# The order of six class bodies behind an expert loop, on one core

## What is computed

```python
logits = (xf @ w_router + b_router)
top_val, top_idx = lax.top_k(logits, 4)          # 4 of 32 experts for each token
top_w = jax.nn.softmax(top_val, axis=-1)
# for each expert e, on the tokens that chose it:
hu = x[toks] @ w_up[e] + b_up[e]                 # 1024 -> 2048
ys = clamped_swiglu(hu) @ w_down[e] + b_down[e]  # 1024 -> 1024
out[tok] += gate * ys
```

## Time and profile before

| | |
|---|---|
| median of 3 runs | 1301.96 us (1298.96 to 1302.73) |
| profiled execution | 1302.53 us, span 1300.2 us |
| TensorE busy (MATMUL) | 1126.4 us, 87% |
| TensorE weight load | 572.4 us, 44% |
| VectorE, ScalarE | 316.0 and 314.6 us, 24% each |
| DMA | 464.88 MB, mean 358 GB/s |
| instruction queues | q8: 30 packets, 0.49 MB; q14: 9 packets, 0.07 MB |

### The profile page before, as it was taken

How to read it: one execution, slowest core, us unless ns; L and a number is a source line. 1 busy time by engine, 2 the same in 40 slices (tenths; PEclk the granted TensorE clock), 3 DMA queues, 4 the chain that set the end, 5 groups by cost and what they waited for, 6 DMA issues and landing times.

```text
span 1300.2 us, 20883 instructions
## 1 busy us (share of the span) xinstructions
PE 1126.4 (87%) x7942; PEld 572.4 (44%) x7943; DVE 316.0 (24%) x802; ACT 314.6 (24%) x589; POOL 0.2 (0%) x4
## 2 busy tenths in 40 slices
PE   6999899997999669988998989989978678687785
PEld 4745688844344334434343333443433333333332
DVE  3045444463112110311211211222111112111112
ACT  2145422132122221112222122231222112221213
POOL 0000000000000000000000000000000000000000
PEclk9999999997999899989999999999999999899898
DMA  9932754453899999559999999999999999999996
GB/s 379 427 125 97 287 230 172 196 217 129 306 390 428 429 427 409 194 193 429 426 428 429 428 428 428 428 428 428 428 429 429 427 430 427 428 428 428 429 429 269
DMA packets 33739, 464.88 MB, mean 358 GB/s; under 512 B 4002, under 2 KB 4130, under 8 KB 5540
## 3 DMA queue, kind: packets, MB, share of 16 engines
q1 hardware_dynamic: 32688, 460.98, 84.7%
q10 hardware_dynamic: 1012, 3.34, 0.6%
HBM read 463.25 MB, written 1.05 MB: 357 GB/s over the span
## 4 chain that ended last, share of the span: by engine, by line
PE 58%; DMA 37%; DVE 2%; issue 2%; ACT 0%; SPq 0%; DVEq 0%; ACTq 0%
DMA ring<-in_w_up 32%; PE psum L973 19%; PE psum L596 17%; PE psum L1050 8%; PE psum L901 4%; DMA ring<-in_w_down 4%; PE psum L965 2%; PE psum L1068 2%; DMA ring<-in_ada_quarters 1%; PE psum L662 1%; DVE area L1756 1%; PE psum L602 1%; PE psum L948 1%; PE psum L1010 0%; PE psum L799 0%
## 5 line engine op out<-in xcount | busy, mean ns | idle before, releaser
L973 PE MATMUL psum<-ring,area 128*32 128x512 f32 (+2 forms) x2432 | 389.0, 628 | 75.7 <-DMA ring<-in_w_up 75.6
L973 PEld LDWEIGHTS psum<-ring,area 128*32 128x32 f32 (+2 forms) x2432 | 107.1, 122 | 347.5 <-issue 226.9
L1050 PE MATMUL psum<-ring,area 128*32 128x256 f32 (+2 forms) x2080 | 191.4, 419 | 24.8 <-DVE area L1741 14.8
L901 PEld LDWEIGHTS psum<-area,x_res 128*128 128x128 f32 x1056 | 125.6, 198 | 34.5 <-issue 34.5
L901 PE MATMUL psum<-area,x_res 128*128 128x128 f32 x1056 | 132.6, 285 | 2.5 <-DVE area L1637 1.7
L1050 PEld LDWEIGHTS psum<-ring,area 128*32 128x32 f32 (+2 forms) x2080 | 75.9, 115 | 129.7 <-issue 66.3
L1263 ACT ACTIVATE area<-area 128x256 f32<-128x256 f32 x51 | 21.3, 417 | 415.4 <-DVE area L1716 415.4
L1716 DVE TENSOR_SCALAR area<-psum 128x256 f32<-128x256 f32 x51 | 21.6, 424 | 400.6 <-PE psum L973 400.6
L1222 ACT ACTIVATE area<-psum,mod,small 128x128 f32<-128x128 f32 (+1 forms) x272 | 101.5, 454 | 60.0 <-PE psum L901 58.6
L1251 ACT ACT_TABLE_LOAD x32 | 41.1, 1283 | 290.2 <-PE psum L948 290.2
L596 PE MATMUL psum<-ring,hT 128*128 128x512 f32 (+1 forms) x192 | 77.5, 559 | 0.0
(11 more groups left out here) (201 smaller groups left out, 655.7 us busy)
## 6 DMA issues: line engine op xcount, KB each, us to landing
ring<-in_w_up SPq DMA_DIRECT2D x128, 2048.0 KB, 22.2
ring<-in_w_down SPq DMA_DIRECT2D x64, 2048.0 KB, 22.5
ring<-in_w_in SPq DMA_DIRECT2D x10, 2048.0 KB, 16.0
ring<-in_ada_w SPq DMA_DIRECT2D x8, 2048.0 KB, 13.7
ring<-in_ada_quarters SPq DMA_DIRECT2D x4, 2048.0 KB, 18.3
ring<-in_w_out SPq DMA_DIRECT2D x2, 2048.0 KB, 9.8
ring<-in_w_in SPq DMA_DIRECT2D x4, 512.0 KB, 19.1
ring<-in_w_branch_b SPq DMA_DIRECT2D x1, 2048.0 KB, 9.3
```

Of the source, the lines that this page charges most:

```text
L901: ins = pe.matmul(ps[banks[i]][:, kk % 4 * P:(kk % 4 + 1) * P], x3[:, tt, kk * P:(kk + 1) * P], S[:, tt, 0:P], start=(tt == 0 and kk % 4 = ...
L973: ins = pe.matmul(ps[b][g * P // G:(g + 1) * P // G, 0:w], XT[:, kk, t0:t0 + P // G], wt[:, c0:c0 + w], start=False, stop=kk == KT - 1, sk ...
L1050: ins = pe.matmul(ps[b][g * M:(g + 1) * M, 0:w], hidT[:, p, q * P + of * M:q * P + (of + 1) * M], down_weights(kk)[:, g * W + d * CW:g * W ...
```

## The change

One tuple gets another order. All bodies, their instructions and the order of the turns stay as they are; only the places of the class bodies in the programs of TensorE, ScalarE and VectorE move. Class 2 (96 tokens) now follows the loop, then class 4 (160), then class 1 (64); classes 3, 5 and 6 stay where they are.

```diff
-BEHIND = (1, 2, 4, 3, 5, 6)
+BEHIND = (2, 4, 1, 3, 5, 6)
```

## The result

The changed kernel takes 1304.91 us (median of 20 runs, 1300.97 to 1313.50), the kernel before 1302.76 in the runs beside it (20 runs, 1298.96 to 1304.22). The ratio is 1.0026, 95% interval 1.0016 to 1.0035: some 3.4 us slower, between 2.1 and 4.6. That is a small loss that the measurement tells from nothing, but it lies inside the band of 0.3% that the prediction called "within", to which it gave 0.35, and not in "slower", to which it gave 0.56. The forecast was 1307.8, in a range of 1300 to 1314.

A forecast was written before the change was run, and what follows sets the result against it. DMA bounds the full stretches; from 309 to 366 us and through turn 6 until 578.7 it waits for TensorE. 4.3 + 1.5 = 5.8 on the profiled 1302.53 gives 1308.3, less 0.6 for the median: 1307.8, range 1300 to 1314.

The forecast's parts named there:

- the change acts through TensorE's fetches alone: Whole kernel: only instruction fetching can act; VectorE's and ScalarE's used bodies fill about a page and add 0 us.
- Turn 0, the same stall: First jump to class 2: goes to page 12 in place of 13, neither fetched yet; same stall, 0 us.
- Turn 2, a new stall: Jump to class 1: page 17 was never fetched, so TensorE stalls anew, 7.2 us with its slow clock.
- Turn 3, the head is gone: Return from class 1: the page with the loop's start was displaced, a second new stall of 7.2 us.
- page n takes the place of page n-8: Instruction memory: eight fixed places; a newly present page, when first entered, fetches its successor even if that is present.
- the ring: Rule formed after measuring: eight places; jumps search all, successors only the next; a missing page goes behind the last used.
- The slack of 9.0 and 10.1 us: Transfers issued at 386.4 and 414.7: 7.2 us delay costs nothing, 14.4 exceeds 10.1, so the DMA idles 4.3 us.
- Turn 6: Class 4: begins in a present page, later fetches page 18 over the loop's start; the return stalls as before, 0 us.
- rival 2: Replacement by order of loading: turns 2 and 3 push out page 14, turn 6 starts stalled, 7.2 more, 1315.0; chance 0.12.
- rival 3: Return from class 4 finds the loop's start, saving 7.2 us: 1294.8 alone (chance 0.07), 1300.6 with the new stalls (0.10).
- Turns 21 to 30: Class 1: four returns stall 7.2 us each; the inner three are covered by 16.2 us slack, the last adds 1.5.
- Rival 1: Class 1 does not push out the loop's start: only the first jump stalls, 7.2 inside 9.0; 1302; chance 0.15.

The follow-up runs named there:

- e1: Against the kernel before: class bodies behind the loop in order 1, 4, 2 (64, 160, 96 tokens) in place of 1, 2, 4; 1299.77 us, ratio 0.9986.
- e3: Against the kernel before: TensorE's program alone in the new order, ScalarE's and VectorE's as before; 1304.83 us, ratio 1.0023.
- f1: Against the kernel before: old order, 153 instructions put in front of TensorE's program, 150 of them never run; 1334.44 us, ratio 1.0238.
- f3: Against the kernel before: class order 2, 5, 1, 4, 3, 6 and 143 instructions in front; 1307.19 us, ratio 1.0027.
- f4: Against the kernel before: class order 3, 2, 4, 1, 5, 6, no instructions in front; 1313.97 us, ratio 1.0082.
- g1: Against the kernel before: class order 4, 2, 1, 3, 5, 6 and 108 instructions in front of TensorE's program; 1297.31 us, ratio 0.9960.
- g2: Against the kernel before: class order 4, 2, 1, 3, 5, 6, no instructions in front; 1299.63 us, ratio 0.9986.
- f2: Against the kernel before: old order, 113 instructions put in front of TensorE's program, 110 of them never run; 1310.23 us, ratio 1.0055.
- e2: Against the kernel before: class bodies behind the loop in order 2, 1, 4 in place of 1, 2, 4; 1302.84 us, ratio 1.0002.
- e4: Against the kernel before: ScalarE's and VectorE's programs alone in the new order, TensorE's as before; 1301.51 us, ratio 0.9997.

## Why the prediction was partly right

- **That the change acts through TensorE's fetches alone: right, shown** by the pair with one engine's order each (1.0023 and 0.9997).
- **Turn 0, the same stall: right.** 3.97 us of issue for 3.74.
- **Turn 2, a new stall of 5.1 plus 2.1 for the clock: place right, size low.** The idle time is 6.60 and the clock takes 2.8, 9.4 in all for 7.2. It was sized from a stall on a partly busy DMA; where the DMA moves over 400 GB/s such a gap is 5.4 to 6.6 us longer than an ordinary one (this kernel, e1, e3, f1, f3, f4, g1 and g2), as the packet itself starts later. The upper bound of the prediction, 6.9, held.
- **Turn 3, the head is gone, a second stall: wrong, and the main error.** The step that failed is "page n takes the place of page n-8, and a page that is newly there fetches its successor, whether that is present or not". It fitted all counts of the kernel before, and so does the ring. They part only in kernels with other orders: no gap at 422, none before turns 25, 28 and 31, 36 packets and not 50 to 60.
- **The slack of 9.0 and 10.1 us: right in kind, about 1 us too long.** The transfer that was issued at 386.4 is issued at 397.1 and lands after 7.7 us, that is, on an idle DMA: its slack was used up. One stall of 9.4 against 9.0 should lose 0.4; the hole in the transfers is 1.3 us, and turns 2 to 5 lost 1.7, where the prediction had 14.4 less 10.1, 4.3. So the mechanism of the term holds, with one stall that is longer in place of two.
- **That also explains the runs' spread,** I think, but it is argued and not shown: a stall just as long as its slack turns each longer fetch into time. The changed kernel's 20 runs span 12.5 us, those of before 5.3; e3 and f3, with the same stall, 7.1 in 12 and 13.1 in ten; g1, without a stall on a full DMA ahead of turn 21, has 1.6 in five runs.
- **Turn 6: entering 17 fetches 18 onto 10 and the return stalls as before: right,** against rivals 2 and 3. No gap stands before turn 6 (0.97 us for 0.99). The 1.6 us that its start lost to the clock were not foreseen. TensorE alone and f2 show a slow L892 too (4.94 and 5.08 us), before, e1, e2, e4, f3, g1 and g2 don't (3.49). What sets it was not tried.
- **Turns 21 to 30: one stall and not four, hidden; the end 0 and not 1.5.** The last turn has its 2.98 us of waiting and 3.33 of products, as before.
- **Sum.** 1.7 + 1.6 in the profile for 4.3 + 1.5 predicted, and 3.4 by the ratio for 5.8. Rival 1 ("only the first jump stalls") was nearer in its mechanism than the forecast; its 1302 was too low, since the one stall was longer than its slack. That the forecast's time came out close is in good part luck: a stall sized too short stood beside one that didn't happen, and 1.6 us of a slow clock in turn 6 that it didn't have stood beside 1.5 at the end that didn't come.
- **Rival 2, replacement in the order of loading,** which the Trainium skill's FIFO (Runtime: NRT & Kernel Launch, Instruction fetch mechanics) would give, has half of the truth. A pure order of loading would have put a gap before turn 6, by the working of that rival, and there is none. But places don't belong to pages either, as 1, 4, 2 shows. The section's window of two pages, out of which a taken branch forces a fetch, is not borne out: in the kernel before, the ten returns from classes 1 and 2, back over up to five pages, have no gap beyond the ordinary 0.5 us, no packet comes from 664 to 1290, and only the return from class 4 stalls.

**Open:** where exactly a missing page is put. The ring is exact in packets and gaps for before, after and six experiments (e1 to e4, g1, g2) and, but for the late successor, f2. In f1 it has the gaps but not the packets, in f3 and f4 neither.

## What to carry to other kernels

When bodies of a run-time choice are longer than the engine's instruction memory, treat their addresses as a schedule. Count the instruction packets by window, find which jump or return shows a gap of "issue" with a clock of 0.50 behind it, and ask of each whether transfers are queued there: under some 16 us of queued work a single gap cost nothing or a few tenths here and a double one 1.5 us, and a gap in a stretch without slack cost 7 us. Then compare several orders and several counts of unused instructions in front, since both move the same page borders, and a rule that fits one kernel's counts can still be the wrong one. And whoever changes any code ahead of such a loop should expect a shift (here up to 2.4%) that has nothing to do with what the code does.

## What the runs showed that was not expected

- 153 instructions that are never executed, in front of TensorE's program, made the kernel 2.4% slower; 108 with the right order made it 0.4% faster.
- A jump to a page that is present, by the ring, can stall too, if its target lies near the page's end and the successor isn't there: 6.19 us in f2's turn 9. In f4 the same shows as a second gap of 1.75 us a few instructions into the body.
- A missing page costs more on a full DMA: 7.2 us of issue in turn 2 of the changed kernel against 3.74 on an idle one at turn 0. Its packet starts 3.9 us after the jump in place of 0.4. The granted clock is 0.50 behind it in both places.
- One stall in a late class 1 turn is followed by none in the next three, though the jumps are the same: by the ring, once the pages stand in another order, they stay.
